# A decoder trunk on one core: one product with ones for the squares, token sums between products, q and k norms from the banks, a reordered start and a head pair begun early

## What is computed

```python
x = x + 0.5 * swiglu(rms_norm(x, ffn_norm[l, 0]), ffn_w_in[l, 0], ffn_w_out[l, 0])
h = rms_norm(x, mix_norm[l])
x = x + (rwkv7_time_mix(h) if l == 0 else dilated_attention_mixer(h, k_sh, v_sh))
x = x + 0.5 * swiglu(rms_norm(x, ffn_norm[l, 1]), ffn_w_in[l, 1], ffn_w_out[l, 1])
if l == 0: k_sh, v_sh = shared_kv(x, kv_norm, w_kv, k_norm)

def rms_norm(x, g):    return x * rsqrt(mean(x * x, axis=-1) + 1e-6) * g
def swiglu(h, wi, wo): gate, up = split(h @ wi); return (silu(gate) * up) @ wo
# in the time mix: kk = k * k_k, divided by its norm over each head of 64
# q and k of the attention: rms_norm over each head of 64, with a gain
```

## Time and profile before

| | before |
|---|---|
| median of 3 runs | 2645.71 us (2644.31 to 2650.67) |
| the profiled execution, its time | 2643.01 us |
| its span, first to last instruction | 2641.3 us |
| granted TensorE clock, mean over the span | 0.971 |
| busy: PE, DVE, ACT, POOL | 2549.0, 805.3, 958.0, 982.9 us |
| share of PE in the chain that ended last | 94% |
| PE waited longest for | x at the start 15.1 us, then w_lo of the first chunk 6.8 us |

### The profile page before, as it was taken

How to read it: one execution, slowest core, us unless ns; L and a number is a source line. 1 busy time by engine, 2 the same in 40 slices (tenths; PEclk the granted TensorE clock), 3 DMA queues, 4 the chain that set the end, 5 groups by cost and what they waited for, 6 DMA issues and landing times.

```text
span 2641.3 us, 47025 instructions
## 1 busy us (share of the span) xinstructions
PE 2549.0 (97%) x18914; PEld 2142.8 (81%) x18930; DVE 805.3 (30%) x1295; ACT 958.0 (36%) x1599; POOL 982.9 (37%) x470
## 2 busy tenths in 40 slices
PE   6999999988998999999999999999999899999999
PEld 5888886767777788888899998888889777888887
DVE  3222014444554232220323012221034366322201
ACT  3222223533554233331434233332144565333321
POOL 3444442431222344444433434444443200444442
PEclk9999998988987899999999999999999999999999
DMA  3333222210000223323233433332232232333321
GB/s 129 96 95 95 96 83 80 92 40 4 5 4 17 75 88 95 95 96 97 94 128 119 160 121 119 95 95 96 96 105 87 65 112 65 97 99 98 95 96 64
DMA packets 180816, 230.39 MB, mean 87 GB/s; under 512 B 16473, under 2 KB 119033, under 8 KB 180665
## 3 DMA queue, kind: packets, MB, share of 16 engines
q1 hardware_dynamic: 180664, 228.20, 27.2%
HBM read 213.47 MB, written 14.68 MB: 86 GB/s over the span
## 4 chain that ended last, share of the span: by engine, by line
PE 94%; ACT 2%; DVE 2%; issue 1%; POOL 0%; SPq 0%; DMA 0%; DVEq 0%; ACTq 0%; POOLq 0%
PE bank L332 21%; PE bank L334 20%; PE bank L333 20%; PE bank L339 6%; PE bank L340 6%; PE bank L341 6%; PE bank L1169 1%; PE bank L1988 1%; PE bank L1282 1%; PE bank L2001 1%; PE bank L1252 1%; PE bank L2024 1%; PE bank L1300 1%; PE bank L1728 1%; PE bank L1484 1%
## 5 line engine op out<-in xcount | busy, mean ns | idle before, releaser
L307 POOL TENSOR_TENSOR w_lo<-w_raw,w_hi 128x1024 fp32r<-128x1024 f32 x376 | 904.7, 2410 | 1390.6 <-ACT w_hi L302 1390.0
L302 ACT ACTIVATE w_hi<-w_raw 128x1024 fp32r<-128x1024 f32 x376 | 395.3, 1058 | 1050.5 <-PE bank L334 876.9
L332 PE MATMUL bank<-xg_hi,w_hi 128*128 128x512 f32 x1408 | 551.0, 391 | 10.1 <-POOL w_lo L307 6.8
L334 PE MATMUL bank<-xg_hi,w_lo 128*128 128x512 f32 x1408 | 549.9, 391 | 0.0
L333 PE MATMUL bank<-xg_lo,w_hi 128*128 128x512 f32 x1408 | 549.7, 390 | 0.0
L332 PEld LDWEIGHTS bank<-xg_hi,w_hi 128*128 128x128 f32 x1408 | 265.6, 189 | 66.6 <-POOL w_lo L307 6.8
L333 PEld LDWEIGHTS bank<-xg_lo,w_hi 128*128 128x128 f32 x1408 | 265.7, 189 | 55.4
L334 PEld LDWEIGHTS bank<-xg_hi,w_lo 128*128 128x128 f32 x1408 | 265.4, 189 | 55.3
L332 PE MATMUL bank<-hid_hi,w_hi 128*128 (+1 forms) x704 | 274.4, 390 | 0.0
L333 PE MATMUL bank<-hid_lo,w_hi 128*128 (+1 forms) x704 | 274.0, 389 | 0.0
L334 PE MATMUL bank<-hid_hi,w_lo 128*128 (+1 forms) x704 | 273.9, 389 | 0.0
(11 more groups left out here) (283 smaller groups left out, 3137.4 us busy)
## 6 DMA issues: line engine op xcount, KB each, us to landing
w_raw<-in_ffn_w_in SPq DMA_DIRECT2D x352, 256.0 KB, 3.0
w_raw<-in_ffn_w_out SPq DMA_DIRECT2D x176, 256.0 KB, 2.7
w_raw<-in_w_kv SPq DMA_DIRECT2D x96, 256.0 KB, 3.1
w_raw<-in_rwkv_w_rkv SPq DMA_DIRECT2D x48, 256.0 KB, 2.9
w_raw<-in_attn_w_q SPq DMA_DIRECT2D x48, 256.0 KB, 3.0
k_dram<-stage SPq DMA_DIRECT2D x6, 1024.0 KB, 4.8
v_dram<-stage SPq DMA_DIRECT2D x6, 1024.0 KB, 5.6
keys<-k_dram SPq DMA_DIRECT2D x24, 256.0 KB, 3.5
```

Of the source, the lines that this page charges most:

```text
L302: act.activation(w_hi[:, s, :], w_raw[:, s, :], ACT.Copy).then_inc(w_hi_ready, 1)
L307: pool.tensor_tensor(w_lo[:, s, :], w_raw[:, s, :], w_hi[:, s, :].bitcast(F32), ALU.subtract).then_inc(w_lo_ready, 1)
L332: pe.matmul(o, hi, x_hi, start=start, stop=False)
L334: return pe.matmul(o, lo, x_hi, start=False, stop=stop)
```

## The change

Six things are joined.

1. **Squares.** In ffn 0, 1, 3 and in `kv` one product with a 128 x 128 tile of ones sums the squares and spreads them over all partitions (`spread_squares_pe`). DVE then adds and takes the reciprocal on 128 x 512 values, ACT the root. In the ffn stages it stands between the two rows of the third chunk, in `kv` behind the first group. The wait of PE for `rstd` ahead of the second group is gone; a wait that bank 7 has been read stands ahead of the fourth tile of a group that uses it.
2. **Token sums.** `kv` and `attn` keep the one-column products for `stat`, one behind each of the 8 tiles of the third chunk. The diagonals and their spreading are gone there (`mix0` keeps them). The ffn stages have no token sums any more.
3. **q and k norms.** ACT squares straight from the bank, DVE multiplies bank, column norm and head norm in one instruction into `raw`; the copy is gone.
4. **Start.** x is loaded first, then chunk 0, then the parameters in 11 + 4 loads, then chunks 1 to 3. ACT splits chunk 0 ahead of the parameters and chunks 1 and 2 between the first tiles of x.
5. **Pair 0 early.** The steps in `EARLY` of pair 0 run inside the v projection on all engines; the layout of SBUF is shifted for that.
6. **End.** x is transposed tile by tile, ACT copies seven of the eight tiles and DVE the last, and three stores take columns 0 to 511, 512 to 767 and 768 to 1023 of all tokens.

```diff
+EARLY = ("zwza", "tw", "ta", "dec", "undec", "pscan", "uscan", "pend", "tk", "kkp", "kk", "kka", "kp", "ara", "arr",
+         "bkb", "bkk", "rk")
...
-            if 0 <= q < pairs:
+            if 0 < q < pairs or q == 0 and kind not in EARLY:
...
+        def mean_square_pe(pe, ph, b):
+            if b == 0:
+                pe.wait_ge(ssq_ready, KT * (ph["ssq"] + 1))
+                pe.wait_ge(x_new, KT * (ph["x"] + 1))
+            ts = slice(b * P, (b + 1) * P) if b < TB else slice(b - TB, T, TB)
+            last = pe.matmul(bank[7][:, b:b + 1], ssq[:, ts], ones[:, 0:1], start=True, stop=True)
+            if b == 2 * TB - 1:
+                last.then_inc(ms_ready, 1)
+        def spread_squares_pe(pe, ph):
             pe.wait_ge(ssq_ready, KT * (ph["ssq"] + 1))
             pe.wait_ge(x_new, KT * (ph["x"] + 1))
+            if ph["cols"] is not None:
+                pe.wait_ge(var_ready, ph["cols"] + 1)
+            pe.matmul(bank[7][:, :], ones[:, :], ssq[:, :], start=True, stop=True).then_inc(squares_spread, 1)
+        def rstd_dve(dve, ph):
+            n = ph["rstd"]
+            dve.wait_ge(squares_spread, n + 1)
+            dve.tensor_scalar(rstd[:, :], bank[7][:, :], 1.0 / D, EPS, ALU.mult, ALU.add).then_inc(rstd_step, 1)
+            dve.wait_ge(rstd_step, 2 * n + 1)
+            dve.reciprocal(rstd[:, :], rstd[:, :]).then_inc(rstd_step, 1)
+        def rstd_act(act, ph):
+            act.wait_ge(rstd_step, 2 * (ph["rstd"] + 1))
+            act.activation(rstd[:, :], rstd[:, :], ACT.Sqrt).then_inc(rstd_ready, 1)
...
+                            if half == 1 and k == 0 and m == 3:
+                                pe.wait_ge(rstd_step, 2 * ph["rstd"] + 1)
...
+                        if first and ph["stat"] is not None and j == 2 and kk == 0:
+                            spread_squares_pe(pe, ph)
...
-                    if first and ph["stat"] is not None:
-                        if j == 2:
-                            mean_square_pe(pe, ph)
-                        if j == 3:
-                            spread_pe(pe, ph)
...
-            pe.wait_ge(rstd_ready, ph["rstd"] + 1)
...
+        def start_load(sp, load_chunks):
+            for b in range(TB):
+                sp.dma_start(x_rows[:, b, :], x_in[0, b * P:(b + 1) * P, :]).then_inc(x_landed[b], 16)
+            load_chunks(range(1))
+            for first, n, v in PAR_LOADS:
...
+            load_chunks(range(1, G_CHUNKS))
...
+            pe.wait_ge(lora_landed, 16 * 6)
+            pe.wait_ge(projection_copied, 8 + 2)
+            zwza_pe(pe, 0, 0)
+            row(2, 0, range(2, 8))
+            after_read(pe, 0, "zw")
+            norms_pe(pe)
+            after_read(pe, 0, "za")
+            row(2, 0, (1,))
+            row(2, 1, range(1, 8))
+            kkp_pe(pe, 0, 0)
+            row(2, 2, range(1, 8))
+            after_read(pe, 0, "kk")
+            for k in range(3):
+                row(2, k, (0,)).then_inc(w_used, 1)
+            for k in range(3, KT):
+                row(2, k, range(8)).then_inc(w_used, 1)
...
                 for b in range(TB):
-                    if n > 0:
-                        act.wait_ge(group_turned, TB * (n - 1) + b + 1)
-                    act.activation(raw[:, b], bank[4 * (gi % 2) + b][:, :], ACT.Copy,
-                                   scale=rs_col(g, b)).then_inc(group_raw, 1)
-                for b in range(TB):
-                    act.wait_ge(group_raw, TB * n + b + 1)
...
-                    act.activation(raw_sq[:, b % 2], raw[:, b], ACT.Square).then_inc(group_squared, 1)
+                    act.activation(raw_sq[:, b % 2], bank[4 * (gi % 2) + b][:, :], ACT.Square,
+                                   scale=rs_col(g, b)).then_inc(group_squared, 1)
...
-                    dve.tensor_tensor(raw[:, b].rearrange("p (h d) -> p h d", d=HD),
-                                      raw[:, b].rearrange("p (h d) -> p h d", d=HD),
-                                      group_stat[:, 3, b * 8:(b + 1) * 8].unsqueeze(2).to_broadcast([P, 8, HD]),
-                                      ALU.mult).then_inc(group_normed, 1)
+                    if n > 0:
+                        dve.wait_ge(group_turned, TB * (n - 1) + b + 1)
+                    dve.scalar_tensor_tensor(raw[:, b].rearrange("p (h d) -> p h d", d=HD),
+                                             bank[4 * (gi % 2) + b][:, :].rearrange("p (h d) -> p h d", d=HD), rs_col(g, b),
+                                             group_stat[:, 3, b * 8:(b + 1) * 8].unsqueeze(2).to_broadcast([P, 8, HD]),
+                                             ALU.mult, ALU.mult).then_inc(group_normed, 1)
...
+        STORES = ((0, 4), (4, 6), (6, 8))
```

More of the change, by code:

```diff
@@ L449, in spread_pe, with columns_dve @@
             last.then_inc(spread_done, 1)
-        def rstd_dve(dve, ph):
-            st = ph["stat"]
-            n, sums_bank = (2 * TB, bank[4]) if ph["ssq"] is not None else (TB, bank[0])
+        def columns_dve(dve, ph):
+            st = ph["cols"]
+            n, sums_bank = (2 * TB, bank[7]) if ph["ssq"] is not None else (TB, bank[0])
             dve.wait_ge(ms_ready, st + 1)
@@ L458, in rstd_dve @@
             dve.reciprocal(stat[:, 1, 0:n], stat[:, 0, 0:n]).then_inc(inv_ready, 1)
+            if ph["ssq"] is not None:
+                return
             dve.wait_ge(root_ready, st + 1)
@@ new lines, in row @@
+            def row(i, k, ms):
+                t = i * KT + k
+                s, slot = (c0 + t) % SLOTS, t % RING
+                pe.wait_ge(w_lo_ready, c0 + t + 1)
+                pe.wait_ge(mix_lo_ready, t + 1)
+                for m in ms:
+                    if k == 0 and i == 0:
+                        if m == 0:
+                            pe.wait_ge(lora_ready, 2)
+                        if m == 1:
+                            pe.wait_ge(lora_gate_added, 1)
+                    elif k == 0:
+                        pe.wait_ge(projection_copied, 8 * (i - 1) + m + 1)
+                    if i < 2:
+                        last = products(pe, bank[m][:, :], s, m * P, mix_hi[:, slot], mix_lo[:, slot], k == 0, k == KT - 1)
+                    else:
+                        last = products_turned(pe, bank[m][:, :], s, m % 2 * 512,
+                                               mix_hi[:, slot, m // 2 * P:m // 2 * P + P],
+                                               mix_lo[:, slot, m // 2 * P:m // 2 * P + P], k == 0, k == KT - 1)
+                    if k == KT - 1 and m < 7:
+                        last.then_inc(projected, 1)
+                return last
@@ new lines, in rwkv_project_pe @@
+            for i in range(2):
+                for k in range(KT):
+                    row(i, k, FIRST_BANKS if i == k == 0 else range(8)).then_inc(w_used, 1)
+            pe.wait_ge(lora_landed, 16 * 6)
[8 more added lines that the diff above has]
+            kkp_pe(pe, 0, 0)
@@ L1356, in z_pe @@
             for hh in range(2):
-                last = pe.matmul(bank[4][rows_of(c, hh), c % 2 * CH:(c % 2 + 1) * CH], ar[head(hh), q % 3, c, 0, :],
+                last = pe.matmul(bank[4][rows_of(c, hh), c % 2 * CH:(c % 2 + 1) * CH], ar[head(hh), 2 - q % 3, c, 0, :],
                                  state[head(hh), c % 2, :], start=False, stop=True)
@@ L1745, in qkv_pe @@
                                 banks_free(pe, ph, gi, b)
+                                if gi == 1 and b == TB - 1:
+                                    pe.wait_ge(var_ready, ph["cols"] + 1)
+                                    if ph["groups"] is KV_GROUPS:
+                                        pe.wait_ge(rstd_step, 2 * ph["rstd"] + 1)
                             ts = tokens(grp[1], b)
@@ L1769, in qkv_act @@
                 last_group = gi == len(ph["groups"]) - 1
+                if ph["groups"] is KV_GROUPS and gi == 1:
+                    rstd_act(act, ph)
                 for j in range(QKV_CHUNKS - last_group):
@@ L2316, in build @@
             ssqs += ph["ssq"] is not None
-            ph["rstd"] = ssqs - 1
+            ph["cols"] = cols if ph["stats"] and "n" not in ph else None
+            cols += ph["cols"] is not None
+            rstds += ph["ssq"] is not None and ph is not attn
+            ph["rstd"] = rstds - 1
             ph["prep"] = p if ph["gain"] else None
```

222 lines of the change are left out of this document (108 added, 114 removed).

## The result

The changed kernel takes 2603.57 us, the median of four runs (2597.70 to 2605.87), against 2648.19 us for the kernel before in four runs beside them (2644.31 to 2653.68). The ratio is 0.9827, with a 95% interval from 0.9801 to 0.9852. The profiled execution spans 2602.0 us, 39.3 us less than before. Predicted were 43.4 us less.

What follows compares the result with a forecast made beforehand. PE, busy 97% of the span, was taken as the bound. Terms summed to -43.4 us: 2599.7 against the profiled 2643.0, or 2602.3 against the runs' median; 2601 was predicted, range 2593 to 2613.

Steps and rivals of the forecast that it cites:

- Start: Kernel start to first block product: loading x first brings that product from 28.3 to 15.6 us, saving 12.7 us.
- Clock of the first products: First block products, at 0.51 clock before: shorter PE idling ahead of them gains 1.0 us, between 0 and 2.3.
- ffn 0: Squares product to second group: token sums, spreading and wait go, a 0.35 us wait for `w_lo` remains; saves 4.95 us.
- ffn 1 and ffn 3: Same stretch, with a table load between root and `w_hi` and about 1.8 us wait; saves 3.8 and 2.3 us.
- kv and attn: Token sums stay at 2.67 us; spreading, wait and slow spell go at full clock; saves 2.7 and 3.5 us.
- q and k norms: Eleven of twelve groups gain nothing; the last group's uncovered chain shortens, saving 1.9 us, from 1.5 to 3.5.
- Pair 0: Projections' end to first masked tile: early preparation leaves DVE's copying of v as bound; saves 11.0 us, 8.5 to 13.
- End: Final transposes and stores: first store barely later, last store some 0.5 us later; costs 0.5 us, from -1 to +1.5.
- clock fall in `kv`, `attn` or behind the waits of 1.54 us: Rival: clock falls in kv, attn, ffn 1 and 3, and first products stay slow; 2608.5 us, chance 0.14.
- stalled projection: Rival: POOL or DVE late in the v projection makes PE wait; 2605 us, or 2612 if all remaining rows starve; chance 0.08.
- half start: Rival: parameter loads or the cold queue decide the start, so only half its gain comes; 2607 us, chance 0.07.
- second drain: Rival: another 1.28 us behind each table load in ffn 1 and 3; 2603.6 us, chance 0.03.

## Why the prediction was right, point by point

2601 us was predicted and 2603.6 measured, inside 2593 to 2613; the forecast case is the one that came. The sum was 4.1 us too large against the profiled execution.

- **Start** (-12.7). -12.58, by the working given: all of x landed just ahead of the 29 transposes at 8.36, `xg_lo` ended 15.62. Two runs show the causes: x behind the parameters costs 4.0 to 5.9 us, the splits behind them 4.5 to 5.9. If the two add up, 1 to 4 us are left. They go with the nine parameter loads that are gone (x was issued at 8.95 us behind 24 of them and at 6.22 behind 15); no run took these back alone. In seven other kernels the product came 0.2 to 1.4 us later, so 15.72 was the early end of a scatter.
- **Clock of the first products** (-1.0). The clock was 1.00 instead of 0.51, but this gave next to nothing. From the first product to T0 pass 15.65 us with the change. In five other kernels with this first group the clock did fall (0.60 to 0.62 over the first 4.28 us), and it took 15.62 to 15.64 us all the same. PE's own work there is 60 products of 0.227 us, 13.6 us: DVE's chain to `ssq` sets T0, and a full clock only makes PE wait for it. Before, 72 products took 18.63 us, 16.3 at the full rate and 2.3 lost to the clock. So the term was priced as PE's time where PE no longer sets the pace.
- **ffn 0** (-4.95). T0 to second group 9.39 us, predicted 9.4. But the two terms of ffn 0 together gave -5.28 and not -5.95: 5.0 behind T0 and 0.3 ahead of it. I had counted the collision of DVE and POOL at the first `xg_lo` only. The start-to-start times of PE show some 2 us of stalls ahead of T0, around the waits for `xg_lo` and `ssq`, which take the place of the slow clock's 2.3. This is the step that was missing.
- **ffn 1 and ffn 3** (-3.8, -2.3). -3.94 and -2.31. T0 to second group 10.76 us against 10.8 in both, behind the load of a table. `w_hi` starts 1.29 us after the load began and 0.02 us lie between root and load. The page that spoke against it (the Trainium skill, ScalarE: Activation LUTs, What ACT_TABLE_LOAD costs) adds a drain of 1.38 us; no row here shows one. Doubling the product showed that this chain sets the time.
- **kv and attn** (-2.7, -3.5). -3.06 and -3.96. The sizes were off by 0.4 us each, since I priced strewn sums like sums in a row (2.67 us); in a row they measure 0.42 us more than strewn. The full clock came, but its 1.6 us in each stage cannot be put down to the strewing alone: with the sums in a row the changed kernel kept the full clock too. The runs bear out that a row can bring a fall and that strewn sums brought none. In these two places a row would have kept the clock as well, so the term was in part lucky.
- **q and k norms** (-1.9). -2.19, and 2.41 in the run that puts the copies back. Eleven groups gave nothing, as predicted; the second product with a column cost DVE 0.23 us for four (2.73 against 2.50), where 0.4 were counted from no row.
- **Pair 0** (-11.0). -9.94, in the run with it late 10.35: inside 8.5 to 13, and nearer to the 10.6 of the chain than to the 11.0 taken. From the last projection product to the first masked tile it is 15.2 us before and 2.5 with the change, the 12.8 of the working; what moved into the projection cost 2.8 us and not 2.2. The 0.4 us that I added for a slow spell behind it did not come; behind `units` the clock falls again. Six of the other kernels had the longer slow spell at the mixer's head and would have shown 8.3 to 8.4. No stall at the fifth `w_lo`.
- **Attention** (no term). +2.06 us in the profiled execution. No edit is there; in ten other kernels of the change the stretch took 176.9 to 179.8 us. It is clock (0.94 over the stretch against 0.96), and chance.
- **End** (+0.5). +1.83, outside the range of -1 to +1.5. The step that failed is "the last store some 0.5 us later". I had looked at when the first store can go and got 0.6 us where 1.11 came, and gave the larger stores of shorter pieces no price at all, where the landing took 0.71 us more. The last store was issued at the same distance from the transposes as before (4.65 us against 4.70); it is its landing that is late.

The 4.1 us between the sum and the profiled execution are the attention's 2.1, which are chance, and sizes that partly cancel: too much was counted for the start of ffn 0, pair 0 and the end, too little for `kv`, `attn` and q.

The rivals: no clock fall in `kv`, `attn` or behind the waits of 1.54 us; no stalled projection; no half start; no second drain; banks of k and q free in time (485.43 us before and after).

## What to carry to other kernels

A queue position can be the wait: when a new, longer chain goes through an engine that also feeds PE, put the feeding instruction ahead of the chain's last step. That was worth 4 us here, together with the table loads that went with it, and cost nothing. Take a chain's cost only where nothing covers it: 29 us of copies in twelve groups were worth 2.4 us, all in the last one. At the end of a program count until the last store has landed: when the first one can go, and into what pieces it is cut. Count a faster clock only where PE sets the pace.

## What the runs showed that was not expected

- **Clock by place.** Eight float32 products of one column in a row, 2.8 us, let the granted clock fall from 2.4 to 1.2 GHz right behind them at some places and not at others, the same places in two executions (0.85, 0.86, 0.85, 0.85, 1.00). The same row in `kv` brought no fall in one kernel and one in another, where it came 7.9 us later. Each fall costs 1.6 us. Strewn among products of 512 columns they cost 0.05 us less each and no fall was seen.
- **DVE beside POOL.** An `ssq` sum took 2.65 us and an `xg_lo` 2.88 us where they take 0.68 and 0.74 alone, each beginning within 0.3 us of a POOL split of 2.4 us and ending 0.55 us behind it. The Trainium skill (SBUF — State Buffer, SBUF: two separate sides) calls it an exclusive lock for the whole instruction; the rows agree. By that rule the start's gain is limited by how many DVE instructions fall on a split. Both orders of the splits that were run had two; an order with none was not run.
- **Stores.** 2 MB in four stores of whole rows ended 6.95 us after the first issue, in three stores of 2 KB and 1 KB pieces 7.66, in four of 1 KB pieces 8.0.
